# Two transformer blocks on one Trainium2 core: u laid out for the state space tile by tile, the third chunk rotated ahead of weight splits, and the root spread before the last gate block

## The reference

```python
h = x @ w_in
u_s5 = h[..., :512]
q = rotary(h[..., 512:768], pos); k = rotary(h[..., 768:1024], pos)
v = h[..., 1024:1536]; gate = h[..., 1536:]
# s5_mixer: a diagonal complex state space over u, then
y = jax.nn.gelu(y)
y = y * jax.nn.sigmoid(y @ glu_w + glu_b)
y_s5 = y * lax.rsqrt(jnp.mean(jnp.square(y), axis=-1, keepdims=True) + LN_EPS) * s5_gain
y_ret = retention(q, k, v, gn_gain) * jax.nn.silu(gate)      # chunked linear attention, 4 heads
x = layer_norm(ALPHA * x + jnp.concatenate([y_s5, y_ret], -1) @ w_out)
```

## Time and profile before

| | |
|---|---|
| time, median of 3 runs | 3396.68 us (3395.66 to 3399.72) |
| profiled execution, its own time | 3388.56 us |
| its span | 3386.7 us |
| PE busy | 3111.3 us, 92% of the span |
| DVE, ACT, POOL busy | 1205.9, 892.8, 1025.9 us |
| granted clock of PE over the span | 0.96 of full |
| chain that ended last | PE 82%, DVE 6%, POOL 4%, ACT 4%, issue 3%, DMA 1% |

### The profile page before, as it was taken

How to read it: one execution, slowest core, us unless ns; L and a number is a source line. 1 busy time by engine, 2 the same in 40 slices (tenths; PEclk the granted TensorE clock), 3 DMA queues, 4 the chain that set the end, 5 groups by cost and what they waited for, 6 DMA issues and landing times.

```text
span 3386.7 us, 35664 instructions
## 1 busy us (share of the span) xinstructions
PE 3111.3 (92%) x14758; PEld 2554.7 (75%) x14758; DVE 1205.9 (36%) x2341; ACT 892.8 (26%) x1318; POOL 1025.9 (30%) x506
## 2 busy tenths in 40 slices
PE   8878899999999989778997887899999999999995
PEld 7767688888888767556876776788887788888884
DVE  8726541221221254562445444312214311111115
ACT  3222332112112133332334444211212411111111
POOL 4333145223223251001332332122122733333332
PEclk9888999999999989889998999999999999999997
DMA  7431111112111121011110010212112111111111
GB/s 177 102 106 53 69 56 53 48 44 69 48 47 50 50 81 40 32 32 38 38 38 32 32 32 31 81 46 73 50 50 93 50 50 63 50 44 50 50 32 50
DMA packets 65328, 188.73 MB, mean 56 GB/s; under 512 B 10416, under 2 KB 19008, under 8 KB 65152
## 3 DMA queue, kind: packets, MB, share of 16 engines
q1 hardware_dynamic: 65168, 186.46, 17.8%
HBM read 163.10 MB, written 23.33 MB: 55 GB/s over the span
## 4 chain that ended last, share of the span: by engine, by line
PE 82%; DVE 6%; POOL 4%; ACT 4%; issue 3%; DMA 1%; SPq 0%; POOLq 0%; DVEq 0%; ACTq 0%
PE PS L367 46%; PE PS L400 8%; PE PS L401 8%; PE PS L402 8%; PE PS L662 3%; PE PS L904 2%; POOL WL L2239 2%; PE PS L793 1%; PE PS L423 1%; DVE s L1504 1%; POOL DD L2412 1%; PE PS L821 1%; PE PS L484 1%; ACT WH L1001 1%; PE PS L702 0%
## 5 line engine op out<-in xcount | busy, mean ns | idle before, releaser
L2239 POOL TENSOR_TENSOR WL<-WR,WH 128x1024 fp32r<-128x1024 f32 x241 | 576.8, 2400 | 2043.1 <-ACT WH L1001 2042.9
L367 PE MATMUL PS<-XH,WH 128*128 128x512 f32 x2176 | 692.2, 400 | 11.8 <-DVE XL L1543 9.1
L367 PE MATMUL PS<-XL,WH 128*128 128x512 f32 x2176 | 678.9, 394 | 0.0
L367 PE MATMUL PS<-XH,WL 128*128 128x512 f32 x2176 | 675.7, 392 | 0.0
L367 PEld LDWEIGHTS PS<-XH,WH 128*128 128x128 f32 x2176 | 405.7, 191 | 101.0 <-issue 17.9
L367 PEld LDWEIGHTS PS<-XL,WH 128*128 128x128 f32 x2176 | 414.5, 190 | 88.4
L367 PEld LDWEIGHTS PS<-XH,WL 128*128 128x128 f32 x2176 | 412.7, 190 | 88.0
L1001 ACT ACTIVATE WH<-WR 128x1024 fp32r<-128x1024 f32 x241 | 253.5, 1055 | 770.6 <-PE PS L402 481.2
L400 PE MATMUL PS<-WH,HH 128*128 128x512 f32 x864 | 339.9, 393 | 14.4 <-POOL HL L2271 14.4
L401 PE MATMUL PS<-WL,HH 128*128 128x512 f32 x864 | 338.7, 392 | 0.0
L402 PE MATMUL PS<-WH,HL 128*128 128x512 f32 x864 | 338.3, 392 | 0.0
(11 more groups left out here) (327 smaller groups left out, 3679.7 us busy)
## 6 DMA issues: line engine op xcount, KB each, us to landing
WR<-in_weights SPq DMA_DIRECT2D x241, 512.0 KB, 3.6
BR<-brbuf SPq DMA_DIRECT2D x12, 512.0 KB, 4.8
RAWX<-in_xT SPq DMA_DIRECT2D x8, 512.0 KB, 7.2
spill<-STQ SPq DMA_DIRECT2D x16, 256.0 KB, 2.3
RX<-in_x SPq DMA_DIRECT2D x8, 512.0 KB, 6.4
xbuf<-XF SPq DMA_DIRECT2D x8, 512.0 KB, 2.6
brbuf<-STG SPq DMA_DIRECT2D x8, 512.0 KB, 2.6
RES<-xbuf SPq DMA_DIRECT2D x8, 512.0 KB, 9.6
```

The costliest lines, as they stand in the source:

```text
L367: last = e.matmul(PS[:, u.b + h, :], w, x[:, k, 512 * h:512 * h + 512], start=k == 0 and w is w1 and x is xh, stop=k == nk - 1 and w is w2)
L2239: e.tensor_tensor(WL[:, v % NSPL, :], WR[:, v % NRAW, :], WH[:, v % NSPL, :].bitcast(F), ALU.subtract).then_inc(w_lo, 1)
```

## The change

The change has three parts.

**u, tile by tile.** The copies to U8 are issued for each tile once its own store has landed, on four semaphores in place of one: 32 DMAs of 64 KB for 8 of 256 KB. The injection now waits for a count of 512.

```diff
-        ub_out, bc_in, u8_in, t8_in = (sem(n) for n in ("u_stored", "s5_tables_landed", "u8_landed", "t8_landed"))
+        bc_in, u8_in, t8_in = (sem(n) for n in ("s5_tables_landed", "u8_landed", "t8_landed"))
+        ub_out = [sem(f"u_stored{p}") for p in range(4)]
@@ inject
-                    e.wait_ge(u8_in, 128)
+                    e.wait_ge(u8_in, 512)
@@ sp_in
+            ubr = D["ubuf"].rearrange("(g c) (j n) -> j c g n", c=16, n=128)
             for p in range(4):
                 u = lots["u", p]
                 load(e, u.units)
                 e.wait_ge(u.drained, u.ndrained)
                 e.dma_start(D["ubuf"].rearrange("(t p) m -> t p m", p=128)[p],
-                            UP[:, p, :, :].rearrange("p j n -> p (j n)")).then_inc(ub_out, 16)
-            e.wait_ge(ub_out, 64)
-            ubr = D["ubuf"].rearrange("(g c) (j n) -> j c g n", c=16, n=128)
-            for jr in range(8):
-                e.dma_start(U8[16 * jr:16 * jr + 16, :, :], ubr[7 - jr]).then_inc(u8_in, 16)
+                            UP[:, p, :, :].rearrange("p j n -> p (j n)")).then_inc(ub_out[p], 16)
+                e.wait_ge(ub_out[p], 16)
+                for jr in range(8):
+                    e.dma_start(U8[16 * jr:16 * jr + 16, 8 * p:8 * p + 8, :], ubr[7 - jr][:, 8 * p:8 * p + 8, :]).then_inc(u8_in, 16)
```

```diff
@@ gpsimd_program
             for i in range(8):
-                if i == 2:
+                if i == 3:
                     pool_cut(e, lots["v", 7].units - 1)
-                if i == 3:
+                if i == 4:
                     pool_cut(e, lots["v", 7].units)
-                if i == 4:
                     pool_cut(e, lots["glu", 1].units)
@@ sp_retention
-            for i in (5, 6, 7):
-                sp_spill(e, "v", i)
+            sp_spill(e, "v", 5)
+            qk(2)
+            sp_spill(e, "v", 6)
+            sp_spill(e, "v", 7)
             load(e, lots["v", 7].units - 1)
-            for i in range(2, 8):
+            for i in range(3, 8):
                 qk(i)
-                if i == 2:
+                if i == 3:
                     load(e, lots["v", 7].units)
```

```diff
@@ root
-                u = claim(e, "rs", 2, at=6)
+                u = claim(e, "rs", 2, at=0)
@@ project
                     e.wait_ge(g_ylo, 4)
+                if i == 4:
+                    e.wait_ge(g_ylo, 8)
@@ the table of steps
-                    7: ((gate, 6), (gate, 7), (root, 0)),
+                    7: ((gate, 6), (root, 0), (gate, 7)),
@@ act_retention
-                    for p in range(4):
-                        e.wait_ge(g_y, p + 1)
-                        e.activation(XH[:, p, :].rearrange("p (n j) -> p n j", j=8), YP[:, p, :].rearrange("p (j n) -> p n j", j=8),
-                                     ACT.Copy).then_inc(g_yhi, 1)
+                    for h in range(2):
+                        for p in range(4):
+                            e.wait_ge(g_y, 4 * h + p + 1)
+                            e.activation(XH[:, p, 512 * h:512 * h + 512].rearrange("p (n j) -> p n j", j=8),
+                                         YP[:, p, :].rearrange("p (j n) -> p n j", j=8)[:, 64 * h:64 * h + 64, :],
+                                         ACT.Copy).then_inc(g_yhi, 1)
@@ normed
+                ps = bank(u, 2).rearrange("p (j n) -> p j n", j=8)
+                for h in range(2):
+                    w = slice(64 * h, 64 * h + 64)
+                    for p in range(4):
+                        y = YP[:, p, :].rearrange("p (j n) -> p j n", j=8)[:, :, w]
+                        e.scalar_tensor_tensor(y, y, cols[:, C_GAIN + p:C_GAIN + p + 1], ps[:, :, w], ALU.mult, ALU.mult).then_inc(g_y, 1)
+                e.wait_ge(g_y, 8)
+                e.tensor_copy(tmp[:, 0:1], PS[:, u.b, 0:1]).then_inc(u.drained, 1)
                 e.wait_ge(lots["g", 7].full, lots["g", 7].nfull)
...
+                for h in range(2):
+                    for p in range(4):
+                        w = slice(512 * h, 512 * h + 512)
+                        e.wait_ge(g_yhi, 4 * h + p + 1)
+                        e.tensor_tensor(XL[:, p, w].rearrange("p (n j) -> p n j", j=8),
+                                        YP[:, p, :].rearrange("p (j n) -> p n j", j=8)[:, 64 * h:64 * h + 64, :],
+                                        XH[:, p, w].rearrange("p (n j) -> p n j", j=8).bitcast(F), ALU.subtract).then_inc(g_ylo, 1)
```

More of the change, by code:

```diff
@@ L1772, in normed @@
                 e.wait_ge(u.full, u.nfull)
-                e.wait_ge(lots["g", 7].full, lots["g", 7].nfull)
[L1774 to L1783, removed]
+                ps = bank(u, 2).rearrange("p (j n) -> p j n", j=8)
[6 more added lines that the diff above has]
+                e.tensor_copy(tmp[:, 0:1], PS[:, u.b, 0:1]).then_inc(u.drained, 1)
+                e.wait_ge(lots["g", 7].full, lots["g", 7].nfull)
+                for h in range(2):
[5 more added lines that the diff above has]
+                                        XH[:, p, w].rearrange("p (n j) -> p n j", j=8).bitcast(F), ALU.subtract).then_inc(g_ylo, 1)
             outs = {9: (0, 1), 10: (2, 3), 11: (4, 5)}
```

## The result

The changed kernel takes 3365.73 us (median of 4 runs, 3365.26 to 3367.49) beside 3396.65 for the kernel before in the same session (4 runs, 3395.66 to 3399.72): ratio 0.9908, 95% interval 0.9891 to 0.9926, 30.9 us faster. The forecast was 3361.0, range 3349 to 3375.

What follows compares the result with a forecast made beforehand. TensorE was taken to bound the kernel, so only its idle time and the slow clock behind it could be won: 10.6 + 21.8 + 3.2 = 35.6 us off the timed median 3396.68, forecast 3361, range 3349 to 3375.

Steps and rivals of the forecast that it cites:

- A: Copying u to U8 tile by tile, 60 to 97 us: first spill lands earlier, TensorE's transposes don't wait; gain 10.6 us.
- B: Third rotated chunk (chunk 2) read and rotated ahead of three weight splits, 204 to 270 us: gain 21.8 us net.
- C: Root before gate 7, scaling in halves, 349 to 386 us: output projection 0 starts on the first half; gain 3.2 us.
- What follows A moves with it: State-space kernels, injection, state scan and outputs hang on TensorE's and ACT's results, so they keep the 10.6 us gain.
- The charge of 1.0 for DVE coming later: Around block 4, DVE comes 1 to 1.5 us later into norm(1), on which glu(2)'s bank depends: 1.0 us off 22.8.
- DVE's work behind it comes 0.5 us later, beside projections 0 and 1: After the second half before output projection 0, DVE's following work shifts 0.5 us, beside projections 0 and 1.
- Rival 1: Collision at 250 us: block 4 or gated output 3 to 4 us late, 6 to 12 us back; 3367 to 3373; chance 0.18.
- Rival 2: Small copies of u don't overlap, so the spill lands after 94 us: gain 25 us, 3372; chance 0.09.
- rival 4: Slower: new copies of u hold SP 2.74 us each, TensorE idles 50 us more, 3422 us; chance 0.02.
- Rival 3: Before output projection 0, halves of strided cuts cost as whole ones, so no gain or reversal: 3364; chance 0.05.
- Later work waits on nothing edited: Behind the edited first 400 us, what is won carries one to one to the kernel's end.
- The 2 to 3 us of wait that the prediction weighed: At the transposes after u's copies: with fixed DMA costs paid serially, spill lands near 86, leaving 2 to 3 us waiting.

Runs made afterwards that it cites:

- the changed kernel on the second chip: The changed kernel itself, unaltered, run again on another chip beside its variants: 3362.33 us, ratio 0.9906 to the kernel before.

## Why the prediction was right, and where it was not

The account of the two profiled executions, in leads: A 10.85; lost to the slow clock behind T8, down to 3.4; B up 21.5 to 24.9; C down 2.5 to 22.4; later work down 1.6 to 20.8, the difference of the spans. The timed difference, 30.9, is 10 us more, since the profiled execution of before lay 8.1 under its median and that of after 1.8 above.

- **A, 10.6 us: right.** 10.85 in the traces, 10.6 timed alone (5.8 to 14.3). The steps came as written: spill issued at 69.58 (near 70) and landed at 72.0 (before 78), no wait at the transposes, no 1.2 GHz behind them. The size hangs on the execution, since the wait that goes was 3.88 to 8.63 us in four traces: the kernels of the state space start at 109.0 to 113.0 us in the four traces without A and at 101.2 to 102.8 in the nine with it.
- **"What follows A moves with it": wrong in this pair of traces, right in the timed runs.** T8's loss was read as absent because one execution of before did not have it. It is in both kernels, so it dropped out of the difference. The forecast of 3361 carried the 8.1 us between profile and median along without knowing what they were. That the changed kernel has this stall too, and so keeps them, was luck.
- **B, 21.8 us: right in the traces.** 26.5 - 3.4 = 23.1 at scores(3), predicted 22.8; 21.5 net. From chunk 2's transposes to scores(3) it took 27.8 us, predicted 28, and chunk 2 was rotated by 210.9 with a lead of 3.4, as computed (214 less the lead). The charge of 1.0 for DVE coming later came out as 1.6, but by other ways: 0.8 at the wait for chunk 4's KZ, and 0.8 in the squares and glu(2), which in this trace ran beside 6.8 us of low clock in place of 3.4. Timed alone, B gave 28.6, and its interval, 23 to 32, does not take in 21.8; A and B together gave 33.1, where the prediction has 10.6 + 21.8 = 32.4.
- **C, 3.2 us: wrong, -2.5 in the traces** (timed, -3.0 alone and -1.2 on top of A and B, neither clear of noise), outside its bounds of 0 to 8.4. The first half of the step is right in kind: XH's first cut still came right behind the fourth weight cut, and TensorE started 6.2 us behind it, predicted 4.9 to 5.1, so 2.4 us were won at its start and not 3.2. The step that failed is "DVE's work behind it comes 0.5 us later, beside projections 0 and 1". It counted DVE's delay against TensorE's results and not against its banks. Projection 1 needs bank 7 from the transposes of chunk 4. Before, the drain (L1803 of that kernel) ended 7.3 us behind projection 0's start, and projection 0, at the low clock, took 8.3. Now projection 0 starts on the first half while DVE still has the second half, the norm and the drain ahead of it, and the drain ends at 357.77, 11.2 us behind the start: the start moved 2.4 us forward and the drain, in the stage's own time, came 1.5 us later. Behind the wait of 3.20 came another 3.4 us of low clock. Moving that one bank gave 4.5 us timed and 7.0 in the traces.
- **Rival 1 (collision in B)** came at its place, with 0.64 us in place of 3 to 4; the prediction's own sign of being wrong, a wait for KZ at block 4, thus turned up, at a size that changed little. **Rival 2** (A fails) and **rival 4** (SP held 2.74 us a copy, slower) are refuted by 0.5 us a copy. **Rival 3** (C gives nothing or reverses) is what happened, by another mechanism: half cuts cost half (7.89 us for eight), and the bank did it. Rival 4 says that the copies of before were held with 1 MB of them queued; in that trace six of 256 KB, 1.5 MB, were issued and not landed.
- **"Later work waits on nothing edited"**: the lead fell from 22.4 to 20.8 behind the edited part, and no experiment looked into that.
- **The level.** The sum of 35.6 less the 5.7 us by which C was missed is 29.9; measured 30.9. With the scatter of single executions, some 10 us, the agreement within 1 us means little.

The Trainium skill (DMA: Bandwidth & Descriptors, Rules for kernel authors) says that many small transfers should be coalesced, and that under 64 KB one pays mostly overhead. The copies here are of 64 KB, at the edge of that. The 2 to 3 us of wait that the prediction weighed came from paying the Trainium skill's fixed 2.0 us per DMA (same page, Anatomy of one DMA, a fit for DMAs that GpSimd issues) one after the other, about 17 us for eight as an estimate. The runs show none of it: the last eight copies, issued by SP, were issued in 3.63 us and had all landed 5.6 us after the first issue, and the wait in A is gone.

## What to carry to other kernels

When work on an engine is split so that a consumer may start sooner, check what else that engine frees behind it, banks above all: the start moves forward and the release does not. A small idle gap is to be priced with the clock behind it: here 1.06 to 3.78 us of idle time ahead of the chain of 128-column matmuls cost 6 to 9 us more, and 2.7 us ahead of 512-column ones 0 to 3. One profiled execution can lack a stall that nearly all others have; when it is well off the timed median, profile again before trusting "no wait here".

## What the runs showed of the hardware

- A gap of 1.06 to 3.78 us in front of a chain of 128-column matmuls was followed, in all ten traces that have one, by 1.2 GHz for the rest of the chain; the clock came back 2.8 to 5.7 us into the next 512-column matmuls (at 149.7 in the changed kernel on the second chip, where these began at 146.92). Beside the gap this cost 6 to 9 us. A gap of 0.59 us, in two traces, was not followed by it.
- A gap of 2.7 us ahead of 512-column matmuls, ending at 119 to 131 us, is in every trace. Behind it came 6.1 us at the low clock in the first trace of before, some 3 in four traces and none in eight. A gap of 1.08 us ahead of 512-column matmuls, near 200 us, was followed by the low clock in four of thirteen traces and cost 1.6 us there.
- Eight copies of 64 KB (0.5 MB) issued behind one another took 3.6 to 4.8 us of SP's queue over all traces with A. One copy of 256 KB, issued with six such copies (1.5 MB) not yet landed, took 2.74 us.
- Ten executions of the same unchanged kernel on one chip lay between 3383.08 and 3398.83 us. The fastest had a mean granted clock of 0.961, the slowest 0.957, so the scatter goes with how often the clock was low.
